# A two-block transformer layer stack on one core: the first mixer worked per token half

## The reference, cut to what matters

```python
def rms_norm(x, g):
    y = xf * lax.rsqrt(jnp.mean(xf * xf, axis=-1, keepdims=True) + EPS)
    return (y * g.astype(jnp.float32)).astype(x.dtype)

def pool_mixer(h, w_grp, scale):           # windows 2, 4, 8, 16; one per group of 256 channels
    ...
        outs.append((upper - lower) / count - hf[:, :, sl])   # causal mean over w tokens, minus h
    y = jnp.stack(outs, axis=2)
    y = jnp.einsum('bsgc,gcd->bsgd', y, w_grp.astype(jnp.float32)).reshape(B, S, D)
    return (y * scale.astype(jnp.float32)).astype(h.dtype)

        h = rms_norm(x, mix_pre_g[layer])
        m = pool_mixer(h, pool_w[layer], pool_scale[layer])
        x = x + rms_norm(m, mix_post_g[layer])
        h = rms_norm(x, mlp_pre_g[layer])
        x = x + rms_norm(sq_relu_mlp(h, w_up[layer], w_down[layer]), mlp_post_g[layer])
```

## Time and profile before

| | |
|---|---|
| median of 3 runs | 1158.08 us (1157.87 to 1158.44) |
| the profiled execution | 1159.37 us, span 1157.4 us from first to last instruction |
| PE busy | 950.6 us (82%) |
| DVE busy | 487.4 us (42%) |
| ACT busy | 382.8 us (33%) |
| DMA | 310.44 MB, 268 GB/s over the span |
| first mixer, up to the first matmul of the MLP | 40.04 us |

### The profile page before, as it was taken

How to read it: one execution, slowest core, us unless ns; L and a number is a source line. 1 busy time by engine, 2 the same in 40 slices (tenths; PEclk the granted TensorE clock), 3 DMA queues, 4 the chain that set the end, 5 groups by cost and what they waited for, 6 DMA issues and landing times.

```text
span 1157.4 us, 14687 instructions
## 1 busy us (share of the span) xinstructions
PE 950.6 (82%) x5903; PEld 710.2 (61%) x5903; DVE 487.4 (42%) x822; ACT 382.8 (33%) x688; POOL 1.9 (0%) x7
## 2 busy tenths in 40 slices
PE   5899999899998999999799888856576666565656
PEld 4789989789767989998688765414132323232321
DVE  3655665755556565566657753210102020101010
ACT  3544554663565554555555430000000000000000
POOL 0000000000000000000000000000000000000000
PEclk9999999999998999999899999978888888887888
DMA  9554546445114355455240885999999999999995
GB/s 354 206 201 163 205 173 202 147 166 216 73 70 167 115 179 215 147 215 194 98 146 1 350 327 207 428 427 429 428 428 429 428 426 430 428 428 429 427 419 210
DMA packets 62737, 310.44 MB, mean 268 GB/s; under 512 B 2528, under 2 KB 3552, under 8 KB 52320
## 3 DMA queue, kind: packets, MB, share of 16 engines
q1 hardware_dynamic: 62256, 308.17, 67.1%
q0 software_dynamic: 432, 1.57, 0.4%
HBM read 308.68 MB, written 1.05 MB: 268 GB/s over the span
## 4 chain that ended last, share of the span: by engine, by line
PE 63%; DMA 22%; DVE 8%; ACT 4%; issue 2%; SPq 1%; DVEq 0%
PE ps L634 14%; DMA ring<-in_w_exp_down 14%; PE ps L636 14%; PE ps L635 14%; PE ps L1084 6%; DMA ring<-in_w_exp_gate 4%; PE ps L1103 4%; PE ps L1065 3%; DMA ring<-in_w_exp_up 2%; PE ps L1115 2%; DVE w_lo L1639 1%; SPq L593 1%; PE ps L836 1%; DVE hT_lo L1620 1%; DVE w_lo L1626 1%
## 5 line engine op out<-in xcount | busy, mean ns | idle before, releaser
L1626 DVE TENSOR_TENSOR w_lo<-ring,w_hi 128x1024 fp32r<-128x1024 f32 x158 | 190.8, 1223 | 84.7 <-ACT w_hi L1209 84.7
L1084 PE MATMUL ps<-ring,x 128*32 128x512 f32 x992 | 126.9, 669 | 83.6 <-DMA ring<-in_w_exp_up 72.9
L1209 ACT ACTIVATE w_hi<-ring 128x1024 fp32r<-128x1024 f32 x158 | 164.5, 1054 | 88.0 <-PE ps L636 82.3
L634 PE MATMUL ps<-hT_hi,w_hi 128*128 128x256 f32 x656 | 187.3, 285 | 4.6 <-DVE hT_lo L1620 2.8
L636 PE MATMUL ps<-hT_hi,w_lo 128*128 128x256 f32 x656 | 186.3, 284 | 0.0
L635 PE MATMUL ps<-hT_lo,w_hi 128*128 128x256 f32 x656 | 186.3, 284 | 0.0
L1084 PEld LDWEIGHTS ps<-ring,x 128*32 128x32 f32 x992 | 38.3, 122 | 166.6 <-issue 166.6
L634 PEld LDWEIGHTS ps<-hT_hi,w_hi 128*128 128x128 f32 x656 | 126.5, 193 | 6.5 <-issue 5.0
L635 PEld LDWEIGHTS ps<-hT_lo,w_hi 128*128 128x128 f32 x656 | 126.5, 193 | 0.5
L636 PEld LDWEIGHTS ps<-hT_hi,w_lo 128*128 128x128 f32 x656 | 126.5, 193 | 0.0
L1103 PE MATMUL ps<-ring,moe 128*32 128x512 f32 x512 | 70.4, 709 | 57.8 <-DMA ring<-in_w_exp_down 56.5
(11 more groups left out here) (281 smaller groups left out, 1218.5 us busy)
## 6 DMA issues: line engine op xcount, KB each, us to landing
ring<-in_w_exp_down SPq DMA_DIRECT2D x32, 2048.0 KB, 20.8
ring<-in_w_exp_gate SPq DMA_DIRECT2D x31, 2048.0 KB, 19.8
ring<-in_w_exp_up SPq DMA_DIRECT2D x31, 2048.0 KB, 22.6
ring<-in_w_up SPq DMA_DIRECT2D x16, 2048.0 KB, 8.1
ring<-in_w_down SPq DMA_DIRECT2D x16, 2048.0 KB, 7.7
ring<-in_w_in SPq DMA_DIRECT2D x6, 2048.0 KB, 8.5
ring<-in_w_kv SPq DMA_DIRECT2D x4, 2048.0 KB, 10.2
ring<-in_w_q SPq DMA_DIRECT2D x2, 2048.0 KB, 9.5
```

What stands on the lines that cost most here:

```text
L634: mm(out, a_hi, b_hi, start=start, stop=False, skip_group_check=True)
L1084: last = mm(wk(side)[q, :], xgT[:, k, q], w4[:, j, k % 2, :] if opening else w[j][:, k, :], start=(k == 0), stop=(k == KD - 1))
L1209: fn(parts(n if edge else None, f)[0].rearrange("p (k w) -> p k w", k=KD), src, ACT.Copy).then_inc(hi_ready, 1)
L1626: ve.tensor_tensor(lo, src, hi.bitcast(F32), ALU.subtract).then_inc(lo_ready, 1)
```

## The change

x is loaded by two DMAs, one for each token half, each with its own semaphore; squares, root, Newton step and scaling are made for half 0 and then for half 1. PE runs 16 matmuls on zeros into banks 4 to 7 as soon as `zero_t` is set. The pooling then accumulates on these zeros: half 0 first, against the 144 columns (`BAND`) in which the band of the pooling matrix can be other than zero, then half 1 against its 128. `yT` is evicted bank by bank, k 0 to 5 by ACT and 6 and 7 by DVE. The channel scale no longer multiplies the projection's result; DVE multiplies it into `pool_w` in its slot, in two instructions of 128x1024, ahead of the projection, and the projection waits for these and for the banks of `yT` group by group. Behind the projection each token half goes through `mix_half` and `mix_add`, which have the form of the later edges. `consts` is issued ahead of chunk 1. No quarter of chunk 1 is split before the sum; quarter 0 is split between the two halves of the activations, quarters 1 to 3 behind them, and the two casts of masks move behind those. `keep_busy` ahead of the transposes of x goes from 14 matmuls before half 0 to 8 before half 1. New semaphores replace `scaled`; their declarations and the bookkeeping of counts are left out here.

```diff
@@ -103,6 +103,7 @@
 PAIR_ITERS = FF // COLS // PAIRS
 QI = 4 * RING
 AHEAD = 2
+BAND = P + max(WINDOWS)
...
 
         @block.sync
         def _(sp):
-            sp.dma_start(x[:, :, :], a["x"][0].rearrange("(s p) d -> p s d", p=P)).then_inc(x_loaded, 16)
+            for s in range(TT):
+                sp.dma_start(x[:, s, :], a["x"][0, s * P:(s + 1) * P, :]).then_inc(x_loaded[s], 16)
             sp.dma_start(kbuf[:, :], a["poolm"]).then_inc(poolm_loaded, 16)
             sp.dma_start(packed[:, :], a["packed"]).then_inc(packed_loaded, 16)
...
@@ -517,8 +527,6 @@
                     sp.wait_ge(lo_ready, split_count(n - RING))
                 sp.dma_start(slot(n)[:, 0:m * w].rearrange("p (m w) -> p m w", m=m), src)\
                   .then_inc(slot_loaded[n % RING], 16)
-                if n == 1:
-                    sp.dma_start(consts[:, :], a["consts"]).then_inc(consts_loaded, 16)
...
@@ -544,7 +552,8 @@
 
             load(N_POOL, *chunk_source(N_POOL))
             sp.dma_start(scale_row[:, :], a["pool_scale"][0].partition_broadcast(P)).then_inc(scale_loaded, 16)
-            sp.dma_start(row[:, :], a["mix_post_g"][0].partition_broadcast(P)).then_inc(scale_loaded, 16)
+            sp.dma_start(row[:, :], a["mix_post_g"][0].partition_broadcast(P)).then_inc(gain_loaded, 16)
+            sp.dma_start(consts[:, :], a["consts"]).then_inc(consts_loaded, 16)
...
 
+            pe.wait_ge(zero_ready, 1)
+            for b in range(4):
+                keep_busy(4 + b, 4)
             pe.wait_ge(poolm_loaded, 16)
+            pe.wait_ge(h_ready, 1)
+            for k in range(KD):
+                mm(wk(k // 2)[:, (k % 2) * T:(k % 2) * T + BAND], h[:, 0, k * P:(k + 1) * P], poolm[:, k // 2, 0, 0:BAND],
+                   start=False, stop=False, skip_group_check=True)
             pe.wait_ge(h_ready, 2)
-            for b in range(4):
-                for k in (2 * b, 2 * b + 1):
-                    for s in range(TT):
-
-                        last = mm(wk(b)[:, (k % 2) * T + s * P:(k % 2) * T + T], h[:, s, k * P:(k + 1) * P],
-                                  poolm[:, k // 2, s, s * P:], start=(s == 0), stop=(s == TT - 1), skip_group_check=True)
-                last.then_inc(yT_banks, 1)
-            arrived(N_POOL)
-            pe.wait_ge(yT_lo, 1)
-            pe.wait_ge(yT_hi, 1)
+            for k in range(KD):
+                last = mm(wk(k // 2)[:, (k % 2) * T + P:(k % 2 + 1) * T], h[:, 1, k * P:(k + 1) * P], poolm[:, k // 2, 1, P:],
+                          start=False, stop=True, skip_group_check=True)
+                if k % 2:
+                    last.then_inc(yT_banks, 1)
             pw = slot(N_POOL)[:, 0:2048].rearrange("p (m w) -> p m w", m=8)
             for s in range(TT):
                 for g in range(4):
+                    if s == 0:
+                        pe.wait_ge(pool_scaled, g // 2 + 1)
+                        pe.wait_ge(yT_lo, g + 1) if g < 3 else pe.wait_ge(yT_hi, 1)
                     for c in range(2):
                         last = mm(acc[:, s, 256 * g:256 * g + 256], yT[:, 2 * g + c, s * P:(s + 1) * P], pw[:, 2 * g + c, :],
                                   start=(c == 0), stop=(c == 1))
...
@@ -749,8 +763,8 @@
                             last.then_inc(half_done, 1)
 
                 for s in range(TT):
-                    if s == layer:
-                        keep_busy(7, (14, 10)[layer])
+                    if s == 1:
+                        keep_busy(7, (8, 10)[layer])
                     turn_half(x, s, x_ready, x_count - 1 + s, 2 * s)
                 if layer == 0:
                     keep_busy(7, 11)
...
@@ -771,8 +785,6 @@
                 down(1, PAIR_ITERS - 1, True)
 
 
-            pe.wait_ge(scaled, 2)
-            pe.wait_ge(zero_ready, 1)
             pe.wait_ge(consts_loaded, 16)
             mlp(0, 0, 2)
 
...
@@ -1226,23 +1238,31 @@
 
             act.preload_act_table_set("natural_log_exp_and_others")
 
-            pre_norm(0)
+            def root(s, ms_sem, count, done):
+                act.wait_ge(ms_sem, count)
+                order(fn(lnv[:, s:s + 1], ms[:, s:s + 1], ACT.Ln))
+                fn(r0[:, s:s + 1], lnv[:, s:s + 1], ACT.Exp, scale=-0.5).then_inc(done, 1)
+
+            for s in range(TT):
+                act.wait_ge(x_loaded[s], 16)
+                fn(h[:, s, :], x[:, s, :], ACT.Square, scale=1.0 / 32, accum_out=ss[:, s:s + 1]).then_inc(first_squares, 1)
+                root(s, first_ms, s + 1, first_r0)
             act.wait_ge(packed_loaded, 16)
-            for k in range(4):
+            for k in range(6):
                 if k % 2 == 0:
                     act.wait_ge(yT_banks, k // 2 + 1)
                 last = fn(yT[:, k, :], wk(k // 2)[:, (k % 2) * T:(k % 2) * T + T], ACT.Copy, scale=poolg[:, k:k + 1])
-            last.then_inc(yT_lo, 1)
-            for f in range(AHEAD):
-                split(1, f, quarter(1, f))
-
-            for s in range(TT):
-                act.wait_ge(scaled, s + 1)
-                sum_squares(mg[:, s, :], s)
-            rsqrt()
-            act.wait_ge(consts_loaded, 16)
-            fn(identr[:, :], ident, ACT.Copy).then_inc(maskr_ready, 1)
-            fn(strictr[:, :], strict, ACT.Copy).then_inc(maskr_ready, 1)
+                if k % 2:
+                    last.then_inc(yT_lo, 1)
+
+            def mix_half(s):
+
+                for half in range(2):
+                    act.wait_ge(quarters_used, 2 * s + 2)
+                    if half:
+                        act.wait_ge(mix_gained, 2 * s + 1)
+                    fn(h[:, s, half * COLS:(half + 1) * COLS], acc[:, s, half * COLS:(half + 1) * COLS], ACT.Square, scale=1.0 / 32,
+                       accum_out=ss4[:, 2 * s + half:2 * s + half + 1]).then_inc(mix_squares, 1)
 
             def edge_to_next(edge, chunks, n, turn, gain, scale, bank=0):
 
...
@@ -1307,10 +1327,17 @@
                     for f in range(4 if j < 3 else 2):
                         step(j, f, PAIR_ITERS - 1)
 
+            for s in range(TT):
+                mix_half(s)
+                root(s, mix_ms, s + 1, mix_r0)
+            act.wait_ge(consts_loaded, 16)
             take_half(0, 0, 0, 0)
-            for f in (2, 3):
+            split(1, 0, quarter(1, 0))
+            take_half(0, 1, 2, 0)
+            for f in (1, 2, 3):
                 split(1, f, quarter(1, f))
-            take_half(0, 1, 2, 0)
+            fn(identr[:, :], ident, ACT.Copy).then_inc(maskr_ready, 1)
+            fn(strictr[:, :], strict, ACT.Copy).then_inc(maskr_ready, 1)
             pre_norm(2)
             mlp(0)
 
...
@@ -1544,20 +1570,6 @@
                 order(ve.scalar_tensor_tensor(rstd[:, :], r1[:, :], 1.5, r0[:, :], ALU.add, ALU.mult))
                 turns[0] += 1
 
-            def normalise():
-                rsqrt()
-                for s in range(TT):
-                    ve.tensor_scalar(h[:, s, :], x[:, s, :], rstd[:, s:s + 1], None, ALU.mult).then_inc(h_ready, 1)
-
-            def add_to_x():
-
-                rsqrt()
-                for s in range(TT):
-                    ve.scalar_tensor_tensor(x[:, s, :], mg[:, s, :], rstd[:, s:s + 1], x[:, s, :], ALU.mult, ALU.add)\
-                      .then_inc(x_ready, 1)
-                xs[0] += 2
-                dve.wait_ge(x_ready, xs[0])
-
             def post_half(edge, chunks, s, scaled2):
 
...
@@ -1641,26 +1653,50 @@
                       .then_inc(lo_ready, 1)
 
             ve.memset(zero_t[:, :].bitcast(F32), 0.0).then_inc(zero_ready, 1)
-            dve.wait_ge(x_loaded, 16)
-            normalise()
+            for s in range(TT):
+                dve.wait_ge(first_squares, s + 1)
+                ve.tensor_scalar(ms[:, s:s + 1], ss[:, s:s + 1], EPS, None, ALU.add).then_inc(first_ms, 1)
+                dve.wait_ge(first_r0, s + 1)
+                newton(s)
+                dve.wait_ge(x_loaded[s], 16)
+                ve.tensor_scalar(h[:, s, :], x[:, s, :], rstd[:, s:s + 1], None, ALU.mult).then_inc(h_ready, 1)
+            dve.wait_ge(scale_loaded, 16)
+            dve.wait_ge(slot_loaded[N_POOL % RING], 16)
+            for part in range(2):
+                w = slot(N_POOL)[:, 1024 * part:1024 * part + 1024].rearrange("p (g c d) -> p g c d", g=2, c=2)
+                scales = scale_row[:, 512 * part:512 * part + 512].rearrange("p (g d) -> p g d", g=2)
+                ve.tensor_tensor(w, w, scales.unsqueeze(2).to_broadcast([P, 2, 2, 256]), ALU.mult).then_inc(pool_scaled, 1)
             dve.wait_ge(packed_loaded, 16)
-            for k in range(4, 8):
-                if k % 2 == 0:
-                    dve.wait_ge(yT_banks, k // 2 + 1)
-                last = ve.tensor_scalar(yT[:, k, :], wk(k // 2)[:, (k % 2) * T:(k % 2) * T + T], poolg[:, k:k + 1], None, ALU.mult)
+            dve.wait_ge(yT_banks, 4)
+            for k in (6, 7):
+                last = ve.tensor_scalar(yT[:, k, :], wk(3)[:, (k % 2) * T:(k % 2) * T + T], poolg[:, k:k + 1], None, ALU.mult)
```

(55 more changed lines are left out.)

## The result

The changed kernel takes **1151.42 us** (median of 4, 1148.78 to 1151.74) against 1158.26 us of the kernel before, measured beside it (4 executions, 1157.87 to 1159.8): a ratio of 0.9932, 95% interval 0.9915 to 0.9949. All ten executions together have a median of 1150.6. Forecast were 1148.8, range 1146.2 to 1151.6: faster as said and inside the range (the first median by only 0.2), but 7 to 8 us gained rather than 9.3. The profiled execution took 1151.26 with a span of 1149.4.

A forecast was written before the change was run, and what follows sets the result against it. Bound: the chain of work before PE's first MLP, with everything behind following its start. MLP start 8.85 us, first quarter 1.55, projection clock -1.1 sum to 9.3: from 1158.08 to 1148.8 us, range 1146.2 to 1151.6.

The forecast's parts named there:

- The bound and the carry: First MLP to experts: loads wait for PE's compute, so starting the first MLP 8.85 us earlier moves everything behind it forward.
- `scale_row` sets the projection: Before the projection: `scale_row` lands at 13.5, DVE multiplies it into `pool_w`, projection starts at 14.9, 3.95 us earlier.
- The batching rule: Loads of x: DMAs should be at least 1 MiB; by it the halves lose about 0.8 us.
- The front part costs and gains nothing: Loads, norm, pooling: pooling ends between 12.3 and 13.5, hidden behind `scale_row`, so none of it sets the end.
- The clock in the projection: Up to 2.6 us idle before the projection lowers TensorE's clock; price between 0 and 1.55 us, taken as 1.1.
- Projection to x: Behind the projection: same sequence as the edge behind attention; x half 0 ready at 22.7, half 1 at 26.65.
- x to the MLP: Transposes, evictions and one split after x half 1: first MLP matmul at 31.2, 8.85 us earlier.
- Splits: Chunk 1's quarters 1 to 3 split behind the MLP's start, covered; chunk 1 lands at 22.3; late first relu also covered.
- The clock at the MLP's start: First MLP quarter: shorter idle before it keeps the clock up, 2.88 us instead of 4.43, gaining 1.55.
- Rival 4: Later edges: one loses its clock, up to 1150.4 us, or one keeps it, 1147.3; chance 0.1, both ways.

The follow-up runs named there:

- e5: Kernel before with more matmuls on zeros filling PE's longer idle stretches at stage edges from 37 to 569 us; 1154.89 us, 0.9969.
- e9: e6 with the pooling matrix packed to the columns that are read, 544 KB instead of 1024 KB ahead of `scale_row`; 1145.48 us, 0.9885.
- e2: Changed kernel without the channel scale: no products of `scale_row` into `pool_w` and no waits for them; 1147.24 us, 0.9910.
- e3: Changed kernel with x in one load again, ACT and DVE waiting for the whole of it; 1148.9 us, 0.9923.
- e4: Changed kernel with the pooling of before, bank by bank after both halves of h, early matmuls on zeros kept; 1149.44 us, 0.9929.
- e1: Changed kernel with 10 more matmuls on zeros between pooling and projection; 1149.0 us, 0.9920.
- e6: Changed kernel with e1's fill and the same matmuls on zeros at the later edges as e5; 1146.74 us, 0.9896.
- e7: e6 with chunk 1 split where it was: quarters 0 and 1 before the sum, 2 and 3 between the activation halves; 1154.61 us, 0.9967.
- e11: Kernel before with 10 more matmuls on zeros ahead of the first MLP only, 21 instead of 11; 1157.53 us, 0.9994.
- e10: e6 without e1's fill, channel scale back on the projection's output half by half instead of in `pool_w`; 1145.07 us, 0.9879.

## Why the prediction was right, and where it was off

- **The bound and the carry.** Right. 667.03 and 666.92 us from the MLP's start to the experts in e5 and e9, in two kernels whose starts lie 10 us apart. In the profiled pair the gain at the experts (8.28) is not smaller than that at the MLP's start (6.94).
- **`scale_row` sets the projection.** Right: released by DVE's product, start at 15.09 against 14.9 and a landing at 13.79 against 13.5. e2 took the wait away and the start moved to 12.26. The loads in halves didn't slow the queue: DVE's product began at 13.59 in e3, with one load, and between 13.48 and 14.12 in the seven profiles with two. The batching rule that the prediction takes from the Trainium skill (DMA: Bandwidth & Descriptors, Bandwidth) has no effect here that these runs show.
- **The front part costs and gains nothing.** Right as to its end, for each part alone (e3, e4). What the sum named but booked at a guess is its side effect, the idle stretch before the projection.
- **The clock in the projection.** It fell, as said, but the price was 1.72 (8.86 against 7.14), not 1.1; e1 got 1.7 back. The step that was mis-sized is the cover: DVE's queue covers nothing of it, since the low stretch (15.8 to 19.2) lay on the first half, whose result the chain waits for. The price even lies above the bound of 1.55. And the reading behind it was too sure: of stretches of 1.9 to 3.8 us the trace of before has nine up to the experts, not seven, and three kept their clock: beside the one before 225.65 also 1.97 us before 301.98 and 1.91 us before 700.45.
- **Projection to x.** Right to the tenth. From the first half's end (20.53, ACT's first square) to the sum's end is 4.11 against 4.04, from sum to sum 3.95 against 3.95.
- **x to the MLP.** Right: 31.3 (e6) where 31.2 without the fall was worked out. In the changed kernel 33.10 against 32.3, 0.2 by the load and 0.6 by the clock.
- **Splits.** Right. Chunk 1 landed at 22.33 in e7, against 22.3; the quarters behind it and the late first relu (37.85) were covered: PE ran 2.9 us per quarter without a pause.
- **The clock at the MLP's start.** The first quarter ran at 1.00 as said. But 1.55 was taken from one profiled execution, which lay 1.3 above the median of the runs, and subtracted from that median. e11's medians give 0.7 to 1.1 for it, with an interval from a loss of 0.5 to a gain of 1.9. So this is likely the second mis-sized term, not shown beyond the noise. With 0.2 for the load, 0.6 for the projection and 0.4 to 0.9 here the 9.3 become about 7.6 to 8.1, and all executions together give 7.6.
- **Rival 4, an edge that turns.** The first profile of the changed kernel lost the clock at both ends of the edge behind the first MLP, before at one. It cost 0.24 (217.23 to 227.38, 10.15, against 9.91 from 225.65 to 235.56), since the wait of 1.05 us for a split at 231.07, which the kernel before has there, vanished in turn. The kernel before:

```profile
231.07 0.50 PE L634 MATMUL ps<-w_hi,hT_hi 128*128 128x512 f32 x1 [1.05 <-DVE w_lo L1626]
...
235.56 0.76 PE L634 MATMUL ps<-edge_hi,hT_hi 128*128 128x512 f32 x1 [1.95 <-DVE hT_lo L1620]
```

## What to carry to other kernels

When a stage becomes one chain, look for the load that ends last and work everything else against that moment: halving loads and products ahead of it only moves idle time about. An in-order engine that waits for a weight chunk holds up all that stands behind it, so prepare weights where they are needed and after they have landed (8 us here). A factor moved from a matmul's result into its weights puts the factor's load ahead of the matmul: compare both orders by when that load lands (e10). And a faster front part can open an idle stretch that lowers TensorE's clock for the matmuls behind it: fill it, or leave the slower order.

## What the runs showed of the hardware that was not expected

- Behind idle stretches of 1.9 to 2.1 us of PE the clock fell in some executions and not in others of the same kernel (behind the first MLP: both lost in one profile of the changed kernel, none in the other), behind 1.5 to 1.7 us it fell at times (before 658 us in e6, not before the projection in e3), and 2.45 us before the pooling in e4 left it up. So the length of one idle stretch doesn't tell by itself. A single profile therefore shows one draw.
- Filling the idle stretches at the edges took 3.3 us off the kernel before and 3.9 off the changed one, for the first less than half of the 7 to 8.5 expected. The profiles of e6 show falls at edges that had kept their clock; that such falls are all of the missing part isn't shown. With the band-packed matrix (e9) the whole way is 1158.2 to 1145.5 us, 1.1%, of which the change itself is 7.6 us.
